# A mixture-of-experts loop over two 32-token groups per round in place of four

## The reference, cut to what matters

```python
logits = tok @ w_router + b_router
top_val, top_idx = lax.top_k(logits, 4)          # 32 experts
top_w = softmax(top_val)
for each expert e, for its tokens:
    hgu = tok @ w_gu[e] + b_gu[e]                # 1024 -> 2048
    gate = min(hgu[:, 0::2], 7); up = clip(hgu[:, 1::2], -7, 7)
    act = (up + 1) * gate * sigmoid(1.702 * gate)
    out[token] += weight * (act @ w_down[e] + b_down[e])
```

## Time and profile before

| | us |
|---|---|
| three runs, median | 1455.91 |
| lowest, highest | 1449.88, 1459.27 |
| the profiled execution | 1459.03 |
| its span | 1457.2 |
| TensorE busy | 1155.9 |
| TensorE weight loads busy | 565.9 |
| VectorE, ScalarE busy | 249.9, 243.9 |

### The profile page before, as it was taken

One profiled execution on the slowest core, in us unless ns is written; L12 is line 12 of the kernel. 1 busy time (PEld: TensorE's weight loads), 2 busy tenths in 40 slices (PEclk: granted clock), 3 DMA queues, 4 the chain that ended last, 5 costly groups with the idle time before them and its releaser, 6 DMA issues.

```text
span 1457.2 us, 21376 instructions
## 1 busy us (share of the span) xinstructions
PE 1155.9 (79%) x8763; PEld 565.9 (39%) x8764; DVE 249.9 (17%) x663; ACT 243.9 (17%) x600; POOL 18.5 (1%) x26
## 2 busy tenths in 40 slices
PE   8999999999778688668775776797658777697866
PEld 4655768884423233232321321333114232233212
DVE  3335243632410101011010100111000010010100
ACT  2134422540111011111110101111011111011101
POOL 1000010000000000000000000000000000000000
PEclk9999999999788789889898887899888989897987
DMA  9833363233996987699899699849997999978595
GB/s 347 309 107 116 110 237 116 77 116 123 382 407 264 424 367 309 281 422 375 353 420 426 281 427 425 340 162 424 424 425 327 424 419 424 421 304 363 227 426 241
DMA packets 66384, 457.96 MB, mean 314 GB/s; under 512 B 7285, under 2 KB 13017, under 8 KB 33433
## 3 DMA queue, kind: packets, MB, share of 16 engines
q1 hardware_dynamic: 65528, 454.18, 76.6%
q0 software_dynamic: 256, 0.79, 0.1%
q10 hardware_dynamic: 448, 0.60, 0.1%
HBM read 454.50 MB, written 1.05 MB: 313 GB/s over the span
## 4 chain that ended last, share of the span: by engine, by line
PE 63%; DMA 24%; issue 10%; DVE 2%; ACT 1%; SPq 0%; ACTq 0%; DVEq 0%
PE bank L1035 18%; DMA ring<-in_w_down 16%; PE bank L1062 10%; DMA ring<-in_w_gu 8%; PE bank L584 6%; PE bank L724 6%; PE bank L1002 5%; PE bank L1010 3%; PE bank L1021 2%; PE bank L633 2%; PE bank L920 2%; PE bank L886 2%; PE bank L573 1%; PE bank L1045 1%; PE bank L610 1%
## 5 line engine op out<-in xcount | busy, mean ns | idle before, releaser
L1035 PE MATMUL bank<-ring,sp_ 128*32 128x512 f32 x3072 | 411.5, 658 | 132.7 <-issue 78.0
L1062 PE MATMUL bank<-ring,mq 128*32 128x256 f32 x3072 | 197.9, 411 | 61.0 <-DMA ring<-in_w_down 60.3
L1035 PEld LDWEIGHTS bank<-ring,sp_ 128*32 128x32 f32 x3072 | 95.3, 116 | 362.1 <-issue 281.3
L1062 PEld LDWEIGHTS bank<-ring,mq 128*32 128x32 f32 x3072 | 102.7, 117 | 169.6 <-DMA ring<-in_w_down 78.3
L1801 DVE TENSOR_SCALAR sp_<-bank 128x256 f32<-128x256 f32 x48 | 20.4, 425 | 842.9 <-PE bank L1035 842.9
L1348 ACT ACTIVATE mq<-bank 32x256 f32<-32x256 f32 x192 | 72.0, 375 | 328.0 <-PE bank L1062 326.3
L1002 PE MATMUL bank<-sp_,sc 128*128 128x128 f32 x384 | 71.0, 370 | 66.2 <-issue 66.2
L1002 PEld LDWEIGHTS bank<-sp_,sc 128*128 128x128 f32 x384 | 68.8, 282 | 77.1 <-issue 77.1
L584 PE MATMUL bank<-ring 128*128 128x512 f32 x192 | 83.2, 592 | 0.0
L724 PE MATMUL bank<-ring 128*128 128x256 f32 x320 | 71.3, 381 | 0.0
L1341 ACT ACTIVATE mq<-bank 128x256 f32<-128x256 f32 x48 | 18.4, 384 | 301.9 <-PE bank L1045 231.5
(11 more groups left out here) (307 smaller groups left out, 739.7 us busy)
## 6 DMA issues: line engine op xcount, KB each, us to landing
ring<-in_w_gu SPq DMA_DIRECT2D x128, 2048.0 KB, 22.8
ring<-in_w_down SPq DMA_DIRECT2D x64, 2048.0 KB, 14.9
ring<-in_w_in SPq DMA_DIRECT2D x13, 2048.0 KB, 10.5
ring<-in_w_out SPq DMA_DIRECT2D x2, 2048.0 KB, 8.5
ring<-in_w_mem_kv SPq DMA_DIRECT2D x2, 1024.0 KB, 6.9
ring<-in_w_mem_kv SPq DMA_DIRECT2D x1, 2048.0 KB, 8.3
ring<-in_cmp_w_k SPq DMA_DIRECT2D x1, 2048.0 KB, 8.5
ring<-in_cmp_w_v SPq DMA_DIRECT2D x1, 2048.0 KB, 8.1
```

What stands on the lines that cost most here:

```text
L1035: mm = nc.tensor.matmul(BH[n % 2][32 * s:32 * s + 32, :], xgT[:, k, 32 * n:32 * n + 32], w[:, c, 512 * s:512 * s + 512], start=k == 0, sto ...
L1062: mm = nc.tensor.matmul(BG[32 * s:32 * s + 32, 0:256], actT[n % 2][:, o:o + 32], w[:, 2 * c + two, 256 * s:256 * s + 256], start=d + c + t ...
```

## The change

A round of the loop takes two items (a pair) in place of four. The number of items is padded to a multiple of two, with the one possible empty item at seat 27, so 46 items in 23 pairs run with these inputs. The gather is 16 matmuls of 64 columns per pair. The scatter runs once a pair; its 128 rows are now two items of 64 rows, where the two halves (two) of the down sum stay apart and are added by the scatter, since Gw repeats the 32 columns. Down is 16 matmuls of 512 columns, evicted by two instructions of 64 x 512. The packed number holds three seats (left, right and the item before), so TensorE loads one per pair. Seats and ring order stay.

```diff
-QUAD = 4
-QUADS = ITEMS // QUAD
-PADS = (3, 5, 27)
+PAIRS = ITEMS // 2
+PAD_AT = 27
@@ gather
                     if half and not first:
-                        pe.wait_ge(S("y_evac"), j * QUAD - 1)
+                        pe.wait_ge(S("y_evac"), j * 2 - 1)
...
-                            mm = nc.tensor.matmul(b[:, P * c:P * c + P], x2[:, t, o:o + P],
+                            mm = nc.tensor.matmul(b[:, 64 * c:64 * c + 64], x2[:, t, o:o + P],
@@ down
-                            for s in range(4):
-                                mm = nc.tensor.matmul(BG[32 * s:32 * s + 32, 0:256], actT[n % 2][:, o:o + 32],
-                                                      w[:, 2 * c + two, 256 * s:256 * s + 256],
-                                                      start=d + c + two == 0, stop=d + c + two == 3, skip_group_check=True)
+                            for hh in range(2):
+                                mm = nc.tensor.matmul(BG[64 * hh + 32 * two:64 * hh + 32 * two + 32, :], actT[n][:, o:o + 32],
+                                                      w[:, 2 * c + two, 512 * hh:512 * hh + 512],
+                                                      start=d + c == 0, stop=d + c == 2, skip_group_check=True)
@@ TensorE, the round
-            def quad(j, first=False):
-
-                pack = pe.value_load(idx[0:1, bass.ds(j + AT_PACK, 1)], min_val=0, max_val=NE ** QUAD - 1)
-                at_seat = [(pack >> (5 * n)) & 31 for n in range(QUAD)]
+            def pair(j, first=False):
+
+                pack = pe.value_load(idx[0:1, bass.ds(j + AT_PACK, 1)], min_val=0, max_val=NE ** 3 - 1)
+                left, right, before = pack & 31, (pack >> 5) & 31, pack >> 10
+                i = j * 2
+                gather(j, first)
+
+                def left_group(row):
+                    pe.wait_ge(S("g_evac"), j * 2 + 1)
+                    up(0, left, 0, row)
+                    bias(0, row)
+                    if not first:
+                        turn(i - 1, 1, j - 1)
+                    up(1, left, 0, row)
+                    pe.wait_ge(S("g_evac"), j * 2 + 2)
+                    if not first:
+                        down(i - 1, before, 1)
+                    up(2, left, 0, row)
+                    up(3, left, 0, row)
+
+                def right_group(row):
...
+                    turn(i, 0, j)
...
+                    down(i, left, 0)
...
+                with pe.If((left & 1) > 0):
+                    left_group(1)
+                with pe.Else():
+                    left_group(0)
                 if not first:
...
+                    pe.wait_ge(S("y_evac"), j * 2)
+                    pe.wait_ge(S("st_evac"), j)
+                    scatter()
+                with pe.If((right & 1) > 0):
+                    right_group(1)
+                with pe.Else():
+                    right_group(0)
@@ ScalarE, results
-                for s in range(4):
-                    ins = nc.scalar.activation(y_sb[32 * n:32 * n + 32, 256 * s:256 * s + 256], BG[32 * s:32 * s + 32, 0:256],
-                                               ACT.Copy)
-                ins.then_inc(S("y_evac"), 1)
+                nc.scalar.activation(y_sb[64 * n:64 * n + 64, 0:512], BG[0:64, :], ACT.Copy)
+                nc.scalar.activation(y_sb[64 * n:64 * n + 64, 512:1024], BG[64:P, :], ACT.Copy).then_inc(S("y_evac"), 1)
@@ VectorE, packing and one-hots
+            step(V.scalar_tensor_tensor(out=packed[:, 1:], in0=seat_row[:, 0:PAIRS - 1, 1], scalar=float(NE * NE), in1=packed[:, 1:],
+                                        op0=ALU.mult, op1=ALU.add))
...
-                V.tensor_tensor(Gw, slots(), slot_of(j), ALU.is_equal).then_inc(S("Gw_made"), 1)
+                V.tensor_tensor(Gw, slots(64), of_pair(rank_it, j, 64), ALU.is_equal).then_inc(S("Gw_made"), 1)
```

More of the change, by code:

```diff
@@ L178, in const_table @@
     add("seat", np.tile(np.array(SEATS, np.float32), (P, 1)))
-    later = [sum(m > x for x in PADS) for m in range(NE + 1)]
+    later = [m > PAD_AT for m in range(NE + 1)]
     add("later", np.tile(np.array(later[:NE] + later[1:], np.float32), (P, 1)))
-    add("pack", np.tile(np.float32(NE) ** np.arange(QUAD, dtype=np.float32), (P, 1)))
+    add("pack", np.tile(np.float32(NE) ** np.arange(2, dtype=np.float32), (P, 1)))
     return np.concatenate(cols, 1), parts
@@ L328, in hybrid_layer @@
         r_f, r_B, r_g, r_M, r_nm = (rows[:, 256 * n:256 * n + 256] for n in range(5))
[L331 to L337, removed]
+        Gm = sp_[:, 0:128].rearrange("p (i g n) -> p i g n", i=NT, g=2)
+        Gw = sp_[:, 128:384].rearrange("p (i g n) -> p i g n", i=NT, g=2)
+        STs = sp_[:, 384:640]
+        xgT = sp_[:, 640:1152].rearrange("p (c n) -> p c n", c=KT)
+        gt = [sp_[:, 1152 + 256 * b:1408 + 256 * b] for b in range(2)]
+        ut = [sp_[:, 1664 + 256 * b:1920 + 256 * b] for b in range(2)]
+        sg = [sp_[:, 2176 + 256 * b:2432 + 256 * b] for b in range(2)]
         y_sb = mq[:, 0:1024]
@@ L361, in hybrid_layer @@
         AA = bg1[0:32, 1544:1545 + 2 * NE]
[L362 to L365, removed]
+        few = bg1[0:32, 1920:1920 + PAIRS]
+        pairs = bg1[0:32, 1960:1961]
+        total = bg1[0:32, 1962:1963]
+        pad = bg1[0:32, 1964:1965]
         starts = bg1[0:32, 1640:1640 + 2 * NE]
@@ L1065, in down @@
                     mm.then_inc(S("down_done"), 1)
-            def quad(j, first=False):
-                pack = pe.value_load(idx[0:1, bass.ds(j + AT_PACK, 1)], min_val=0, max_val=NE ** QUAD - 1)
-                at_seat = [(pack >> (5 * n)) & 31 for n in range(QUAD)]
-                if not first:
[L1072 to L1104, removed]
@@ L1106, in _ @@
             pe.wait_ge(S("x2_ready"), 2)
             pe.wait_ge(S("idx_ready"), 1)
[L1108 to L1111, removed]
+            last_pair = pe.value_load(idx[0:1, AT_LAST:], min_val=NE // 2 - 1, max_val=PAIRS - 1)
+            pair(0, first=True)
+            with pe.Fori(1, last_pair + 1) as j:
+                pair(j)
@@ L1116, in _ @@
                                      b_dn[:, 512 * hh:512 * hh + 512], start=False, stop=False, skip_group_check=True)
[L1117 to L1120, removed]
+            last_seat = (pe.value_load(idx[0:1, bass.ds(last_pair + AT_PACK, 1)], min_val=0, max_val=NE ** 3 - 1) >> 5) & 31
+            turn(last_pair * 2 + 1, 1, last_pair)
+            pe.wait_ge(S("y_evac"), last_pair * 2 + 1)
+            down(last_pair * 2 + 1, last_seat, 1)
             pe.wait_ge(S("last_y"), 1)
@@ L1346, in results, with pair @@
                 act.wait_ge(S("down_done"), i * 2 + 2)
[L1347 to L1352 removed]
+                nc.scalar.activation(y_sb[64 * n:64 * n + 64, 0:512], BG[0:64, :], ACT.Copy)
+                nc.scalar.activation(y_sb[64 * n:64 * n + 64, 512:1024], BG[64:P, :], ACT.Copy).then_inc(S("y_evac"), 1)
+            def pair(j, first=False):
                 tokens(j)
                 if not first:
[L1355 to L1366 removed]
+                    results(j * 2 - 1, 1)
+                gates(j * 2, 0)
+                results(j * 2, 0, None if first else j)
+                gates(j * 2 + 1, 1)
+            act.wait_ge(S("idx_ready"), 1)
+            last_pair = act.value_load(idx[0:1, AT_LAST:], min_val=NE // 2 - 1, max_val=PAIRS - 1)
+            pair(0, first=True)
+            with act.Fori(1, last_pair + 1) as j:
+                pair(j)
+            results(last_pair * 2 + 1, 1)
             nc.scalar.activation(sg[0][:, 0:1], sg[0][:, 1:2], ACT.Copy).then_inc(S("last_y"), 1)
@@ L1738, in _ @@
             step(V.tensor_copy(total, bank("first")[0:NE, 2 * NE:2 * NE + 1]))
-            fours = C("iota")[0:NE, :].rearrange("p (k four) -> p k four", four=QUAD)[:, :, 0]
-            step(V.tensor_scalar(few, fours, total, None, ALU.is_lt))
-            step(V.tensor_reduce(quads, few, AX.X, ALU.add))
-            step(V.scalar_tensor_tensor(out=pad, in0=quads, scalar=float(QUAD), in1=total, op0=ALU.mult, op1=ALU.subtract))
+            twos = C("iota")[0:NE, :].rearrange("p (k two) -> p k two", two=2)[:, :, 0]
+            step(V.tensor_scalar(few, twos, total, None, ALU.is_lt))
+            step(V.tensor_reduce(pairs, few, AX.X, ALU.add))
+            step(V.scalar_tensor_tensor(out=pad, in0=pairs, scalar=2.0, in1=total, op0=ALU.mult, op1=ALU.subtract))
             step_read(V.scalar_tensor_tensor(out=starts, in0=C("later")[0:NE, :], scalar=pad, in1=bank("first")[0:NE, 0:2 * NE],
@@ L1807, in activate, with pair @@
                 V.scalar_tensor_tensor(out=u, in0=u, scalar=1.0, in1=g, op0=ALU.add, op1=ALU.mult).then_inc(S("act_ready"), 1)
-            def quad(j, first=False, final=False):
+            def pair(j, first=False, final=False):
                 if not final:
@@ L1812, in quad @@
                     onehot(j + 1)
-                activate(j * QUAD, 0)
+                activate(j * 2, 0)
                 if not first:
-                    dve.wait_ge(S("a_full"), j * QUAD)
```

(14 more changed lines are left out.)

77 lines of the change are left out of this document (35 added, 42 removed).

## The result

The changed kernel takes 1381.6 us (median of 4 runs, 1379.0 to 1385.1) against 1455.6 us (4 runs, 1449.9 to 1459.3): 0.950 of the time before, with an interval of 0.946 to 0.954. The forecast was 1459 us and no change. What came is the first rival: the small loop stays loaded in TensorE. Its price, 1394 us, was still 14 us too high for the profiled run, which took 1380.0 us (span 1378.2).

What follows compares the result with a forecast made beforehand. Neither TensorE nor DMA bounds alone. TensorE's work: +58 + 37 - 24 - 15 - 16 = +40 us; at the end -5 and +5 give 0, so 1459 us, no change; range 1392 to 1486.

Steps and rivals of the forecast that it cites:

- balance of the kernel before: Expert phase: neither side bounds alone; DMA idles some 115 us, TensorE waits 115 us for weights and 159 for issue.
- rival C: TensorE's gather: a matmul of 64 columns halves it, 23 x 2.3 = 53 us less work; 1441 us, chance 0.08.
- The scatter: TensorE, once a pair: 23 for 12, 23 x 3.9 = 90 us against 53.0, so +37 us.
- VectorE and ScalarE hidden: One-hots half as wide and two evictions for four stay behind the group's later matmuls: 0 us.
- Down at nothing: TensorE's down: 16 x 512 columns stream as long as 32 x 256; 0 us, bounds -6 and +6.
- walk over idle DMA: Weight transfers followed seat by seat through the expert phase: the forecast's idle DMA is 110 us against 115.
- rival A: TensorE's small loop stays loaded: 138 us of gaps go, idle DMA falls from 115 to 50; 1394 us, chance 0.22.
- Issue gaps: TensorE's waits at jumps and forks: 121 + 17 = 138 us against 153.5, so -15, and -16 for slow restarts.
- The page that speaks against it: Skill pages on TensorE's instruction store: a two-page window leaves 1459 us, 128 KB alone gives 1394; rows can't decide.
- -24 us of TensorE: Two dummy groups behind seats 3 and 5 go, at 11.9 us each without a gap.
- The work added falls largely where DMA leads: Expert phase: added work mostly hidden, removed work where TensorE leads; -5 us, with +5 for unlucky gaps: 0.
- I take 5.6: One gather on TensorE takes 5.6 us, bounds 3.3 and 6.5: 23 x 5.6 = 129 against 71.0, +58 us.

Runs made afterwards that it cites:

- two loops of four groups: Kernel before with turn and down outside the arms, 1396.7 us; the same with 512-column down matmuls and its loop moved by 132 instructions, 1398.0 us.
- badly placed loop: Changed kernel with turn and down outside the arms and the body written twice, moved by 84 instructions: 1425.1 us, ratio 0.981.
- pair written twice: Changed kernel with its loop body written twice, 11 rounds of two pairs, 1,960 instructions, same work and order: 1430.6 us, ratio 0.982.
- short loop of four: Kernel before with turn and down taken out of the even and odd arms, 48 groups in 12 quads: 1396.7 us, ratio 0.959.

## Why the prediction was wrong

**Right.** The balance of the kernel before, two sides that are late in turn. The size of the new loop ("about 1,000 ... 4 to 5 packets": 982 and 5). The gather: its pace doesn't follow the columns, and the 128x128 loads are what both forms share; a gather of 32 records takes 3.79 us with 64 columns against 3.84 with 128, so rival C is out:

```profile
909.29 3.79 PE L1001 MATMUL bank<-sp_,sc 128*128 128x64 f32 x32
```

The scatter: 87.0 us, against 90. SP at nothing: the DMA share is 1.00 and 1.01 in the windows that the loads lead. VectorE and ScalarE hidden: TensorE waited 0.8 and 1.5 us for ScalarE. Down at nothing at the end, as the two loops of four groups show. The walk over idle DMA: for rival A it gave 17 us at seat 8 and 33 at seat 16; 15 and 32 were measured. For the rest of the phase it gave nothing, and there 11 were measured.

**The step that failed** stands under "Issue gaps": "But it jumps back 21 times for 10", at 5.8 us each, and 17 us of forks behind it. None of the 138 us came: "issue" was 6 us, of which 5.6 lie before the first group. I had read the ten packets of a round as a way of the engine to fetch whatever it jumps to, and took the stalls over two arms as evidence "against" rival A. They are none. A loop of 2,386 instructions in ten packets, run in a circle through a store of eight, finds nothing of itself again if the oldest packet always makes room, and shows the very same rows as an engine that holds only two packets. That reading is an inference; that all nine packets of a loop one too long land again each round agrees with it. The rows of before could not tell these apart, and the prediction said so in "The page that speaks against it". But it then gave A 0.22, where nothing in the trace weighed against it.

By the Trainium skill, Advanced Engine Details and Errata, "ISA Cache", TensorE has 128 KB in lines of 16 KB; the runs agree: seven packets and the next stay, eight and the next don't. The "Only 2 cache lines!" of that section of the Trainium skill, and the two-page window of the Trainium skill, Runtime: NRT & Kernel Launch, "Instruction fetch mechanics", are not what TensorE did here: a jump back over five packets took 213 ns. The measurement decides.

**Terms that were mis-sized.** The gain of rival A, 1459 - 65 = 1394, left out that the packets themselves use the DMA engines (9 us, 0.7% of the span for 0.1%), that the weights' own packets took 6 us less, and 8 us that stay open; its idle DMA, 50 us for 58 measured, erred by 8 the other way. The dummy groups' "-24 us of TensorE" is right, and is 1 us at the end. "The work added falls largely where DMA leads" is half true: of 95 us added to the gathers 38 arrived; of the 78 us that the badly placed loop costs TensorE (48.5 more "issue", 29.4 for gathers behind a jump) 45 did. "I take 5.6" for a gather fits neither kind: it is 3.79 us without a jump, so that the 129 became 90.7, and behind one (126.8 - 12 x 3.79) / 11 = 7.4 us in the pair written twice, the first gather of the phase counted in. So the forecast was too low for its own mechanism too. At the 4.5 to 4.9 us that each of ten jumps back cost at the end (45 and 49 us), 21 of them would have put the changed kernel at 1476 to 1485 us, not 1459; that is an estimate, and no run had a fetch in front of every pair. A slip in the chances: by their own terms they give 0.32 for faster and 0.44 for the same, for 0.31 and 0.45.

**What the change is worth by parts.** The whole is 74 us. With the loop too large for the store and ten jumps back, the same groups, pairs and waits give 25 (1430.6); the other 49 are the store. The split holds for ten jumps back: with the 21 of the changed kernel a refetched loop would be slower still, by the estimate above slower than before. The short loop of four says where the 25 come from: 59 us of the old time went with the long arms, and the pairs give 34 of them back (1430.6 against 1396.7, both with ten jumps back). In these runs gathers and scatters are 126.8 + 86.5 us of TensorE against 67.1 + 46.1, while the pairs have two groups less. The split of the 34 was not tried.

## What to carry to other kernels

Count the instructions of each engine's loop, in packets of 256, and where the loop begins: on TensorE of this chip a loop that lay in up to seven packets stayed loaded and its branch took 0.2 us, and one in eight took 6 us per jump and cost 38 to 45 us in all, with ten jumps. Where both branches of a fork repeat the same code, take it out first: that alone gave 59 us here, and with wider down matmuls and the loop loaded 93 to 97. A trace of a loop that doesn't fit can't tell how much would stay; the distance to the limit has to be tried.

## What the runs showed of the hardware that was not expected

Moving a loop by 84 instructions, with nothing else changed, cost 45 us, and moving it by 244 nothing; moving the other by 132 cost 39. Once a loop is one packet too long all of it goes (100 to 111 packets in 11 rounds), not only what is too much. Code that is jumped over isn't counted by its length: 870 such instructions within the loop left the time as it was (1381.4 us) and the packets at 10 in the phase, against 7. And fetching isn't free for the others: 100 packets of 16 KB took 0.5 to 0.7% of the DMA engines' time in a phase that the loads bound.
